# A decoder layer on one core: projecting token tiles 2 and 3 in the middle of the token loop instead of ahead of it

## What is computed

```python
p = h @ lp['w_in']                                  # RWKV, GDN and gate columns
ya, shift_new, wkv = rwkv_branch(p_rw, shift_prev, wkv0, lp)   # recurrence over tokens
yb, conv_new, ssm = gdn_branch(p_gd, conv_buf, ssm0, lp, chunked)
merged = gates[..., :D_MODEL] * (ya @ w_branch_a) + gates[..., D_MODEL:] * (yb @ w_branch_b)
x1 = layer_norm(DN_ALPHA * x + merged @ w_out, ...)
q = x1 @ wq                                         # then top 16 of 128 by 128 keys, per head
hpre = einsum('tkd,td->tk', u_tab[expert], x1)      # 128 rows of u per token
ff = einsum('tk,tkd->td', gate * gelu(hpre), v_tab[expert])   # 128 rows of v per token
x2 = layer_norm(DN_ALPHA * x1 + ff, ...)
```

## Time and profile before

| what | us |
|---|---|
| three runs, median | 2156.61 |
| lowest, highest | 2156.49, 2164.32 |
| span of the profiled execution | 2167.9 |
| loading and projection (0 to 188.5) | 188.5 |
| recurrence of tile 0 (188.5 to 263.7) | 75.2 |
| rest of the opening (263.7 to 512.5) | 248.8 |
| token loop (512.5 to 2144.3) | 1631.8 |
| tail | 23.6 |

### The profile page before, as it was taken

One profiled execution on the slowest core, in us unless ns is written; L12 is line 12 of the kernel. 1 busy time (PEld: TensorE's weight loads), 2 busy tenths in 40 slices (PEclk: granted clock), 3 DMA queues, 4 the chain that ended last, 5 costly groups with the idle time before them and its releaser, 6 DMA issues. The chain is left out here.

```text
span 2167.9 us, 32130 instructions
## 1 busy us (share of the span) xinstructions
PE 1626.5 (75%) x12765; PEld 974.2 (45%) x12789; DVE 1336.0 (62%) x2996; ACT 398.7 (18%) x754; POOL 1019.4 (47%) x1091
## 2 busy tenths in 40 slices
PE   7998879897978785598888656888776555656555
PEld 7887866864655552065655302666553000100000
DVE  4296177784645458865545777645456875676745
ACT  1321332241222011113401201223012000100000
POOL 0000020004645555665545566645455677777774
PEclk9997999996989996599999756979998555555555
DMA  9214286656999999999999999989999999999997
GB/s 253 77 49 136 80 223 183 225 177 225 358 369 400 399 401 407 377 355 388 394 399 400 412 403 382 383 304 398 399 400 404 401 402 405 406 406 397 406 407 273
DMA packets 271257, 718.93 MB, mean 332 GB/s; under 512 B 29220, under 2 KB 77823, under 8 KB 270075
## 3 DMA queue, kind: packets, MB, share of 16 engines
q0 software_dynamic: 151904, 554.59, 66.3%
q1 hardware_dynamic: 116552, 161.44, 21.7%
q10 hardware_dynamic: 2650, 0.85, 0.2%
HBM read 695.58 MB, written 21.30 MB: 331 GB/s over the span
## 5 line engine op out<-in xcount | busy, mean ns | idle before, releaser
L2558 DVE CUSTOM_DVE_ANT_0 arena<-arena,ps 128x1024 f32<-128x1024 f32 x520 | 634.5, 1220 | 523.1 <-PE ps L2611 331.7
L2458 POOL DMA_INDIRECT arena<-peer_u_dram,arena x520 | 503.2, 968 | 500.6 <-DVE arena L2558 415.9
L2503 POOL DMA_INDIRECT arena<-peer_v_dram,arena x520 | 489.0, 940 | 163.6 <-issue 152.5
L2611 PE MATMUL ps<-arena 48*128 48x512 bf16 x1040 | 264.7, 501 | 338.3 <-DVE arena L2558 325.6
L1318 PE MATMUL ps<-arena 128*128 128x128 f32 (+1 forms) x3072 | 415.7, 291 | 85.9 <-DMA arena<-w_in_dram 35.1
L1318 PEld LDWEIGHTS ps<-arena 128*128 128x128 f32 x3072 | 380.6, 200 | 178.7 <-issue 123.0
L2624 PE MATMUL ps<-arena 128*32 128x512 f32 x2080 | 397.1, 847 | 24.0 <-DMA arena<-peer_v_dram,arena 23.8
L2611 PEld LDWEIGHTS ps<-arena 48*128 48x128 bf16 x1040 | 53.7, 98 | 648.7 <-DVE arena L2558 574.0
L2592 ACT ACTIVATE arena<-arena 128x4 f32<-128x4 f32 x130 | 26.8, 206 | 910.1 <-DVE arena L2558 909.8
L388 PE MATMUL ps<-arena 128*128 128x260 f32 (+1 forms) x704 | 131.7, 349 | 3.9 <-ACT arena L466 3.9
L388 PEld LDWEIGHTS ps<-arena 128*128 128x128 f32 x704 | 116.4, 193 | 18.1 <-ACT arena L466 4.0
(11 more groups left out here) (367 smaller groups left out, 1805.6 us busy)
## 6 DMA issues: line engine op xcount, KB each, us to landing
arena<-w_in_dram SPq DMA_DIRECT2D x40, 1024.0 KB, 13.1
arena<-peer_wq_dram SPq DMA_DIRECT2D x32, 1024.0 KB, 14.6
arena<-w_out_dram SPq DMA_DIRECT2D x16, 1024.0 KB, 15.7
arena<-w_in_dram SPq DMA_DIRECT2D x30, 512.0 KB, 4.1
arena<-peer_u_dram,arena POOLq DMA_INDIRECT x520
arena<-peer_v_dram,arena POOLq DMA_INDIRECT x520
arena<-w_branch_a_dram SPq DMA_DIRECT2D x8, 1024.0 KB, 14.8
arena<-w_branch_b_dram SPq DMA_DIRECT2D x8, 1024.0 KB, 16.7
```

The costliest lines, as they stand in the source:

```text
L2458: pool.indirect_dma_start(m["arena"][:, at:at + D], None, m["a"]["peer_u"][0], offsets(m, k)).then_inc(m["sem"](f"e_u{k % RU // UB}"), 16)
L2503: pool.indirect_dma_start(e["V"][j % RV], None, a["peer_v"][0], offsets(m, j)).then_inc(v_in[j % RV // BATCH], 16)
L2558: dve.tensor_tensor_reduce(u, u, ps[:, 0:2, :], 1.0, 0.0, ALU.mult, ALU.add, e["hp"][:, c:c + 1]).then_inc(sem("e_h"), 1)
L2611: mm = pe.matmul(ps[:, h, :], e["pick"][r, i:i + 1].to_broadcast([3 * GROUP, P]), e["xp"][r, g % 2, :], start=True, stop=True)
```

## The change

Only tokens 0 to 255 and the samples are projected ahead of the loop, GDN and RWKV columns alike (264 columns, `TA`). The late projection goes. x of tokens 256 to 511 is loaded on ACT's queue, transposed inside tile 0's recurrence (`extra_*`, with the small b and a columns of these tokens) and put into `fin_dram`. Tile 1's inputs go from SBUF to `finbuf` directly. In the token loop a new set of streams, `second_*`, projects tokens 256 to 511 (tiles 2 and 3) between tokens 95 and 142: 30 units of 128 columns, one every 1.4 tokens, with all of DVE's work on them (convolution, mixing, norms, decays) 256 tokens wide, and writes the results to `fin_dram` for both tiles. Their weights come in 15 slabs of 1024 rows by 256 columns (ring of 4). Tile 2's load waits for the end of that, and tile 2 begins at token 141 instead of 118, in a shorter time (`STRETCH` 0.86). Other edits: the selector constants are replaced by a broadcast identity column, keep masks are set by POOL and DVE instead of loaded, a part of the samples' due times lies earlier, and tile 0's choice has a pace of 0.4.

```diff
-BEGINS = (-160.0, 3.0, 118.0, 244.0)
-STRETCH = (1.0, 1.0, 1.0, 1.07)
-CHOOSE_PACE = (0.55, 0.58, 0.78, 0.78, 1.2)
+BEGINS = (-160.0, 3.0, 141.0, 249.0)
+STRETCH = (1.0, 1.0, 0.86, 1.02)
+CHOOSE_PACE = (0.4, 0.58, 0.56, 0.7, 1.2)
...
+GROUPS = (("gk", 4), ("gq", 4), ("gv", 4), ("z", 4), ("wg", 2), ("k", 4), ("r", 4), ("v", 4))
+SB, UNIT = 95.0, 1.4
+SSLOTS = 4
+def unit_at(g, ct):
+    return SB + UNIT * (unit_number(g, ct) - 1)
...
+def second_sp(m, sp):
+    def slab(s):
+        g, h = SECOND_SLABS[s]
+        c0 = GROUP_ROW[g] * P
+        if s >= SSLOTS:
+            sp.wait_ge(sem("p_mm"), 2 * (s - SSLOTS) + 2)
+        src, here = a["w_in"][0, :, c0 + 256 * h:c0 + 256 * h + 256], shaped(flat(f["ring"][s % SSLOTS]), [KD, 256])
+        sp.dma_start(here, src.rearrange("(k p) c -> p k c", p=P)).then_inc(slabs[s % SSLOTS], 16)
...
+    yield front_at(1, "rows") + 0.3
+    m["fs"].wait(sp, 2, "rows", 0)
+    for s in range(SSLOTS - 1):
+        slab(s)
+    yield front_at(1, "store") + 0.1
+    sp.wait_ge(sem("x1_saved"), 16 * 13 * 2)
+    for n in (2, 3):
+        sp.dma_start(f["x"][:, :, (n - 2) * P:(n - 1) * P], fin_rows(m, n, "x", KD)[:, :, 0:P]).then_inc(sem("p_x"), 16)
+    slab(SSLOTS - 1)
...
+def second_pe(m, pe):
...
+                if u == 1 and h == 0:
+                    pe.wait_ge(sem("p_x"), 32)
+                    mm = pe.matmul(ps[:, FB + u % 2, 0:NF], w, f["x"][:, 4 * h + k], start=(h == 0 and k == 0), stop=(h == 1 and k == 3))
...
+def second_dve(m, dve):
+    def keys():
+        yield unit_at("k", 3) + 1.4 * UNIT + 0.8
+        dve.wait_ge(sem("p_spilled_gg"), 32)
+        st.link(dve.tensor_tensor(scr, kk, kk, ALU.mult))
...
+    yield SB - 0.5
+    dve.wait_ge(sem("p_x"), 32)
+    st.link(dve.memset(keep, 1.0))
...
 def fin_sp(m, sp, n):
-    yield front_at(n - 1, "fin")
+    yield front_at(n - 1, "fin") if n > 2 else unit_at("v", 3) + 6.8
     m["fs"].wait(sp, n, "rows", 0)
+    if n == 2:
+        second_done(m, sp)
...
-            in_turn(front_sp(m, sp, 0), store_sp(m, sp, 0), sample_sp(m, sp), late_sp(m, sp))
+            in_turn(front_sp(m, sp, 0), spill_sp(sp), store_sp(m, sp, 0), sample_sp(m, sp))
...
-            in_turn(recur_r_pe(m, pe, 0), recur_g_pe(m, pe, 0), front_pe(m, pe, 0), sample_pe(m, pe), late_pe(m, pe))
+            in_turn(recur_r_pe(m, pe, 0), recur_g_pe(m, pe, 0), extra_pe(m, pe), front_pe(m, pe, 0), sample_pe(m, pe))
...
-            in_turn(experts_dve(m, dve), *(s(m, dve, n) for n in later for s in (recur_r_dve, recur_g_dve, front_dve)),
+            in_turn(experts_dve(m, dve), second_dve(m, dve), *(s(m, dve, n) for n in later for s in (recur_r_dve, recur_g_dve, front_dve)),
```

More of the change, by code:

```diff
@@ L216, in program @@
             m[name] = late.take(shape, dt)
[L217 to L232, removed]
+        m["arena"], m["rings_at"] = arena, late.at
+        small_at = expert_rows(m)[2]
+        fin_at = ARENA - NFIN * (P + NS)
+        high = Space(arena, small_at + SMALL, fin_at)
+        for name, n in (("Praw", RT_), ("sw", 4), ("aa", 4), ("G", 4), ("Gi", 4), ("mix", RT_), ("kk", 4), ("scr", 4), ("xT", KD), ("gg", 4),
+                        ("rawA", QT), ("sqA", 8), ("convA", QT), ("zA", ZT)):
+            m[name + "_at"] = high.at
+            m[name] = high.take([P, n, TA])
+        m["Gp"] = m["sw"]
+        m["once_at"] = high.at
+        m["finbuf"] = arena[:, fin_at:ARENA]
+        second = Space(arena, fin_at, ARENA)
+        for name, shape in (("xrowB", [P, 2, D]), ("xTB", [P, KD, NF]), ("wba", [P, KD, BG]), ("lin", [BG, NF]), ("spB", [BG, NF]), ("keep", [P, 2, NF])):
+            m[name] = second.take(shape)
+        early = Space(arena, low.at, small_at)
         m["tmp"] = lambda name, shape, dt=F32: early.take(shape, dt)
@@ L336, in _ @@
         def _(dve):
[L337 removed]
+            for n in range(2):
                 dve.wait_ge(turned, n + 1)
@@ L485, in _ @@
             tiles(6)
[L486 to L493 removed]
+            act.wait_ge(unit_mm, 1)
@@ L512, in _ @@
             tiles(11)
-        @block.gpsimd
-        def _(pool):
-            nc.gpsimd.memset(bg[:], 0.0).then_inc(bg_zero, 1)
         @block.vector
@@ L1270, in front_sp @@
                 sp.wait_ge(m["sem"]("q_kmm"), 2)
-            elif before == "f":
+            else:
                 source, g, h = SLABS[j]
@@ L1707, in opening_buffers @@
+    m["samples"] = s
+    rest = Space(space.arena, own.at, end)
+    f.update(qT=rest.take([P, HP * P]), left=rest.take([P, D]), parts=rest.take([P, 3, D], BF16),
+             scores=shaped(past_mix, [HP, NK]), x1row=past_mix[:, HP * NK:HP * NK + D])
     f["choose"] = {}
@@ new lines, in chain, with merged, extra_pe @@
+def chain(*streams):
+    for s in streams:
+        yield from s
+def merged(*streams):
+    heads = [next(s, None) for s in streams]
+    while any(h is not None for h in heads):
+        i = min((i for i, h in enumerate(heads) if h is not None), key=lambda i: heads[i])
+        yield heads[i]
+        heads[i] = next(streams[i], None)
+def extra_pe(m, pe):
+    ps, sem = m["ps"], m["sem"]
+    yield begins(0) + 4.0
+    pe.wait_ge(sem("xB_in"), 32)
+    for n in range(2):
+        for k in range(KD):
+            mm = pe.transpose(ps[:, 2 * n + k // 4, (k % 4) * P:(k % 4 + 1) * P], m["xrowB"][:, n, k * P:(k + 1) * P], const(m, "ident"))
+            if k % 4 == 3:
+                if k == 7:
+                    mm.then_inc(sem("xB_mm"), 1)
+                yield begins(0) + 4.5 + 1.0 * n + 0.5 * (k // 4)
+    yield begins(0) + 8.0
+    pe.wait_ge(sem("xB_out"), 2)
+    for k in range(KD):
+        mm = pe.matmul(ps[0:BG, 0, 0:NF], m["wba"][:, k, :], m["xTB"][:, k, :], start=(k == 0), stop=(k == KD - 1))
+    mm.then_inc(sem("xB_ba"), 1)
```

978 lines of the change are left out of this document (536 added, 442 removed).

## The result

| | before | after |
|---|---|---|
| median of the runs made side by side, us | 2160.47 (2156.49 to 2171.74) | 2235.02 (2231.91 to 2237.35) |
| span of the profiled execution, us | 2167.9 | 2235.5 |
| ratio of the times | | 1.0336, 95% interval 1.0293 to 1.0378 |

What follows compares the result with a forecast made beforehand. PE and DVE were taken to bound the kernel up to 512.5 us, DMA the tokens after. Front terms of -68 and token terms of +94 gave +26: span 2194, time about 2183 us (+1.2%), range 2126 to 2224.

Steps and rivals of the forecast that it cites:

- Projection, -30: First projection stage: fewer columns shorten DVE's chain, which ends the stage; 30 us less, bounds -22 and -38.
- Recurrence, +8: Tile 0's recurrence: added transposes, matmuls and evictions on a nearly full PE cost 8 us, bounds +3 and +14.
- Opening, -46: Rest of the opening before the first token: the late projection leaves, 46 us less, bounds -36 and -55.
- Tokens 91 to 143, +89 (66 + 9 + 14): Token loop with the moved projection: 66 us for bytes, 9 for DVE, 14 for the wait for x.
- not the bound: PE in the token stretch: 178 us of work in about 235, so PE does not set the pace.
- The wait for x: PE and DVE near token 95: a 26 us stall for x's load, of which the rings cover 12; 14 lost.
- Tile 2's wait, +5: Near token 143: a stall of 10 to 20 us for tile 2's load, 12 covered by the rings; 5 us lost.
- From span to time: Whole kernel: 11.3 us taken off the forecast span of 2194 to get the time, about 2183.
- (1): Rival for the token loop: only bytes count, rings swallow the waits, DVE keeps up; time 2134, faster; chance 0.22.
- (2): Rival: opening as forecast, +68 us in the tokens, gain and price cancel; time 2157; chance 0.2.
- (3): Rival: the opening gives less, first dot product at 466, tokens as forecast; time 2205; chance 0.13.
- (4): Rival: transfers reach line rate from 512 B on, so added bytes cost 57 us, not 72; time 2168; chance 0.05.

Runs made afterwards that it cites:

- e10: Changed kernel plus 192 small matmuls with unread results, strewn over the end of the opening to keep PE busy; ratio 1.0412 to the kernel before.
- e9: Kernel before with only the token loop's new places for tiles 2 and 3 (tile 2 at token 141, tile 3 at 249); ratio 0.9979.
- e1: Changed kernel without 7/8 of the rows of slabs 4 to 14, 10.1 MB less to load; ratio 1.0293 to the kernel before.
- e2: Changed kernel without 6 of the 8 matmuls of each unit of the second projection; ratio 1.0338 to the kernel before.
- e13: Changed kernel with fewer slab rows, matmuls, DVE steps and spill rows, x loaded early, tile 2 at token 148; ratio 0.9982 to the kernel before.

## Why the prediction was wrong, step by step

The span came 41.5 us above the forecast's 2194. The step that failed with the most weight is the loop's: that DMA paces the tokens, so that DVE's and PE's new work mostly fits beside the bytes (66 for bytes, 9 for DVE, nothing for PE) and the rings cover 12 us of each wait (14 for x, 5 for tile 2). The runs showed in its place that the in-order lists of DVE and, for some tokens, of PE set the pace, and that both waits cost their full length. Two front terms, the projection's and the opening's, were taken too large as well. The terms, as the prediction set them; the rest of the 52 us between 2183 and 2235 is the last point.

- *Projection, -30: measured -20.9.* "What ends the stage is DVE" holds for the changed kernel. The term that failed is DVE's saving, "about half of its 75 us go": its chain from 113 to the end went from 75.7 us (112.95 to 188.64) to 54.3, which is 21.4 and not 36. The RWKV columns were halved, but I had not counted that the GDN columns nearly double, and with them the GDN norm's reciprocal (13.35 + 6.75 after, 7.0 + 13.2 before, no gain at all). The lower bound, -22, came near by luck: its reason, "PE becomes the end", is not what happened.
- *Recurrence, +8: measured -1.6.* The new steps fitted into PE's and DVE's gaps (PE is busy 67.8 of 73.6 us now, 64.1 of 75.2 before). That is outside its bounds (+3 and +14), to the good.
- *Opening, -46: measured -32.6.* The choice went as forecast, its start to the turn about 63 us instead of 68. The 82 us ahead of the queries became 64 (302.5 to 366.4), not 53: I took away the late steps and left the rest as fast as it had been, but the rest ran on a PE that now waits and has a lower clock; how much each of the two did stays open (e10). And behind the choice DVE waits 17.09 us for the first spread, where 23.2 less 13 are 10. The late z columns were not all of that wait: with them gone, PE stands idle before its first spread while the first gathers run:

```profile
456.73 0.61 PE L2808 MATMUL ps<-arena 48*128 48x512 bf16 x2 [15.58 <-PEq L2382]
```

- *Tokens 91 to 143, +89 (66 + 9 + 14): measured +102.6, against e9 114.2.* Near in size by luck, wrong in cause. It is not the bytes: e1. In tokens 95 to 115 DVE's new work is laid end to end with what DVE did there already (38 us more of DVE, 43 us more of time), not hidden behind transfers. "At the 0.88 that DVE has reached" was the mis-step. That row had DVE at 0.88 with DMA full; it does not say that 78 us more fit beside DMA. "From 118 on DVE is free again" holds, but there PE's list, which "not the bound" had dismissed by its average, holds up the spreads (35 us more in tokens 115 to 130), and the spill of gg that "the rings cover" is waited for, 4.6 us (in e2 another spill, 14.1). The wait for x cost 23 us, not 14: tokens 91 to 95 took 41.4 us against 18.3 in e9, and nothing behind them won it back.
- *Tile 2's wait, +5: measured about +29.* Against e9, which has the same places, tokens 143 to 170 take 102.1 instead of 73.3. I let the rings cover 12 us of the stall and forgot that the move by itself brings 24 us there, which the stall eats; the 21 us that the move puts into tokens 170 to 290 stay. Seen from the kernel before, this shows as +25.3 over tokens 143 to 290, the largest single miss of the sum.
- *Tokens 0 to 91* took 4.7 us less, for no reason that was tested; e9, which leaves these tokens as they were, took 3.8 less.
- *From span to time.* I took 11.3 us off because the profiled execution of before stood that far above its median. After, they are 0.5 apart. The distance belonged to that one execution, not to the kernel.

The sign came out as forecast, but for other reasons than those given. Of the rivals, (1), only bytes count, is refuted from the other side: in the kernel as it stands bytes hardly count, the waits, DVE and PE do. (2), gain and price cancel, is refuted by the time. (3), the opening gives less, came true in its first half (the way to the queries gave 18 us instead of 29, and the wait at its end is 17, as it had it), together with a costlier loop; the first dot lay at 457, before its 466. (4) had the time at 2168 and falls with it; its rule was not put to the test.

What stays open in part: 203.9 us in e13 against 149.6 in e9. Bytes would explain some 21 of the 54 us if DMA were the bound, but its share is 0.92, and DVE's waits for gathers in the stretch, in e9 and then in e13, say that it is not:

```profile
DVE arena L2558 <- DMA arena<-peer_u_dram,arena: 15.5, 11, 2.6
```

```profile
DVE arena L2761 <- DMA arena<-peer_u_dram,arena: 0.8, 1, 0.8
```

DVE is busy 40.5 us more than in e9 and idles 13.8 more; for gathers it hardly waits any longer, but 7.8 us for x and 20.7 for PE's spreads (16.5 in e9), the rest for ACT and a spill. How much of the 54 us would go with each of these was not tried.

## What to carry to other kernels

When work is moved into a loop that a transfer paces, ask which engine's list has to carry it in order, and ask it for short stretches and not for the average: DVE was 75% busy beside a full DMA queue here, and yet most of its new work came on top (35 us taken off again gave 28, 20 gave 13), because in the 20 tokens where half of it was put DVE was 90% busy already. A wait put into two in-order lists cost its full length here, though the rings held several tokens of data, and what the move had won around it besides. An experiment that frees one engine can show nothing because another wait takes its place; look in its trace for what the freed time became. A wide reciprocal on DVE is worth a look: 512 elements took 3.35 us, a product of the same width 0.69. The Trainium skill ("VectorE: DVE Perf Modes", section "🔬 Walkthrough: the 8-slice pipeline in each mode") says that Reciprocal is an iterated division with a repeat count of 8, which points the same way as this ratio of 4.9 but does not give its size.

## What was not expected of the hardware

The granted clock of PE in two stretches of the opening was 0.76 and 0.85 instead of 1.00 after the late projection had gone, that is, when PE had less to do between its waits; the same query matmuls then took 8.79 us instead of 7.38. With filler matmuls between them the clock was 1.00 again. Work taken from PE made the work that was left slower here.
